# Expert output rows kept in DRAM per pass and fetched per token in the last pass, in a two-layer trunk

## What is computed

```
for l in range(2):
    x = x + hybrid_mixer(rmsnorm(x, attn_norm[l]), ...)
    h = rmsnorm(x, ffn_norm[l])
    if l == 0: x = x + (silu(h @ w_gate) * (h @ w_up)) @ w_down        # width 2816
    else:
        top_logit, top_e = top_k(h @ w_router + b_router, 2)           # 8 experts
        top_w = softmax(top_logit)
        for each token t, each of its two experts e with weight w:      # width 1408
            x[t] += w * ((silu(h[t] @ w_gate[e]) * (h[t] @ w_up[e])) @ w_down[e])
```

## Time and profile before

| | |
|---|---|
| median of 3 runs | 1048.85 us (1046.59 to 1050.11) |
| the profiled execution | 1049.15 us, its span 1047.4 us |
| mean granted PE clock | 0.998 of 2.4 GHz |
| busy PE, DVE, ACT, POOL | 98%, 80%, 62%, 3% of the span |
| DMA | 248.74 MB, mean 237 GB/s |
| HBM read, written | 246.99 MB, 1.05 MB |
| passes 0 to 7 of the experts | about 632 to 1037 us of the span |

### The profile page before, as it was taken

How to read it: one execution, slowest core, us unless ns; L and a number is a source line. 1 busy time by engine, 2 the same in 40 slices (tenths; PEclk the granted TensorE clock), 3 DMA queues, 4 the chain that set the end, 5 groups by cost and what they waited for, 6 DMA issues and landing times.

```text
span 1047.4 us, 14339 instructions
## 1 busy us (share of the span) xinstructions
PE 1026.5 (98%) x5058; PEld 867.8 (83%) x5058; DVE 833.5 (80%) x1165; ACT 653.0 (62%) x896; POOL 27.9 (3%) x75
## 2 busy tenths in 40 slices
PE   7999999999999999999999999999999999999997
PEld 6888788878888897888888877889888988898885
DVE  5799887765554556689887768999999999999986
ACT  6658655554343444657655556776877677777864
POOL 6000000040000000000000000000000000000000
PEclk9999999999999999999999999999999999999999
DMA  9735545675655554634555476999999989998992
GB/s 269 239 107 187 172 155 189 213 243 182 203 187 187 195 181 130 199 101 161 170 172 174 147 281 205 313 356 329 334 360 335 352 306 368 341 348 304 380 336 86
DMA packets 115093, 248.74 MB, mean 237 GB/s; under 512 B 4913, under 2 KB 29555, under 8 KB 115041
## 3 DMA queue, kind: packets, MB, share of 16 engines
q1 hardware_dynamic: 113040, 243.55, 67.7%
q0 software_dynamic: 2000, 4.51, 1.8%
HBM read 246.99 MB, written 1.05 MB: 237 GB/s over the span
## 4 chain that ended last, share of the span: by engine, by line
PE 87%; DVE 7%; ACT 2%; DMA 2%; issue 1%; SPq 0%; DVEq 0%; ACTq 0%
PE bank L369 26%; PE bank L371 26%; PE bank L370 26%; DVE wlo L357 2%; DMA ring<-in_w_in 2%; PE bank L981 1%; ACT whi L350 1%; DVE dacc L1593 1%; DVE h L1387 1%; PE bank L920 1%; DVE x L1385 1%; PE bank L917 1%; PE bank L941 1%; PE bank L942 1%; DMA ring<-in_moe_w_gate 1%
## 5 line engine op out<-in xcount | busy, mean ns | idle before, releaser
L357 DVE TENSOR_TENSOR wlo<-ring,whi 128x1024 fp32r<-128x1024 f32 (+2 forms) x506 | 540.1, 1120 | 94.1 <-ACT whi L350 92.0
L350 ACT CAST whi<-ring 128x1024 fp32r<-128x1024 f32 (+2 forms) x506 | 462.7, 972 | 86.3 <-PE bank L371 75.0
L369 PE MATMUL bank<-whi,hTh 128*128 128x512 f32 (+3 forms) x992 | 376.2, 379 | 2.7 <-DVE hTl L1362 1.3
L371 PE MATMUL bank<-whi,hTl 128*128 128x512 f32 (+3 forms) x992 | 370.9, 374 | 0.0
L370 PE MATMUL bank<-wlo,hTh 128*128 128x512 f32 (+3 forms) x992 | 370.6, 374 | 0.0
L369 PEld LDWEIGHTS bank<-whi,hTh 128*128 128x128 f32 x992 | 186.8, 188 | 34.0 <-issue 2.0
L371 PEld LDWEIGHTS bank<-whi,hTl 128*128 128x128 f32 x992 | 186.6, 188 | 29.2
L370 PEld LDWEIGHTS bank<-wlo,hTh 128*128 128x128 f32 x992 | 186.9, 188 | 28.5 <-issue 0.5
L369 PE MATMUL bank<-whi,oTh 128*128 128x512 f32 x392 | 155.0, 395 | 0.0
L371 PE MATMUL bank<-whi,oTl 128*128 128x512 f32 x392 | 153.0, 390 | 0.0
L370 PE MATMUL bank<-wlo,oTh 128*128 128x512 f32 x392 | 152.8, 390 | 0.0
(11 more groups left out here) (301 smaller groups left out, 736.2 us busy)
## 6 DMA issues: line engine op xcount, KB each, us to landing
ring<-in_w_in SPq DMA_DIRECT2D x40, 1024.0 KB, 5.2
ring<-in_moe_w_down SPq DMA_DIRECT2D x40, 1024.0 KB, 6.6
ring<-in_moe_w_gate SPq DMA_DIRECT2D x32, 1024.0 KB, 7.7
ring<-in_moe_w_up SPq DMA_DIRECT2D x32, 1024.0 KB, 8.5
ring<-in_moe_w_gate SPq DMA_DIRECT2D x16, 768.0 KB, 7.8
ring<-in_moe_w_up SPq DMA_DIRECT2D x16, 768.0 KB, 4.5
ring<-in_ffn_w_gate SPq DMA_DIRECT2D x11, 1024.0 KB, 5.1
ring<-in_ffn_w_up SPq DMA_DIRECT2D x11, 1024.0 KB, 5.3
```

The lines of the kernel that those rows point to most:

```text
L350: nc.scalar.copy(whi[pc.part(hf)][:, 0:n], pc.raw[:, hf * n:(hf + 1) * n]).then_inc(hi_done, 1)
L357: nc.vector.tensor_tensor(wlo[q][:, 0:n], pc.raw[:, hf * n:(hf + 1) * n], whi[q][:, 0:n].bitcast(F32), ALU.subtract).then_inc(lo_done, 1)
L369: nc.tensor.matmul(o, sh, wh, start=start, stop=False)
L371: return nc.tensor.matmul(o, sl, wh, start=False, stop=stop)
```

## The change

The expert's output rows of a pass are no longer multiplied back to tokens in the next pass. ACT copies banks 0 and 1, without weights, into `ystage` (the tile `gain`, free by then), and SP writes it (512 KB) to a tensor in DRAM, between the fetches of pieces 7 and 8 of the next pass. POOL first fills the rows of passes 7 to 11 with ones (five DMAs), and in the last pass, once the rows of pass 6 have landed, fetches each token's two rows by four indirect DMAs of 128 rows of 4 KB, into the tiles `htokh` and `htokl` (free by then). DVE adds them to `x` with the tokens' weights (`add_rows`). For that it computes each token's row numbers and weights in pass 0 (`token_rows`, 17 instructions; a row that the last pass makes gets the weight 0 here). Only the last pass still goes through slot_rows, rows_upper, rows_lower, scatter and scattered.

```diff
@@ tiles (build_trunk)
+        hotw = place("hotw", [P, MT, NE])
...
+        rowmark = place("rowmark", [P, 1])
@@ aliases and the tensor in DRAM
+        ystage = gain
+        yrows = nc.dram_tensor("yrows", (PASSES * P, D), F32).ap()
+        ypass = yrows.rearrange("(e p) d -> e p d", p=P)
+        tokrow = [[t[:, m, :].bitcast(F32) for m in range(MT)] for t in (htokh, htokl)]
@@ SP
-            def expert_stream(p, e):
+            def expert_stream(p, e, first=False):
...
+                    if j == ERING + 2 and not first:
+                        sp.wait_ge(y_hi, 2 * p)
+                        sp.dma_start(ypass[bass.ds(p - 1, 1), :, :].rearrange("e p d -> (e p) d"),
+                                     ystage[:, :]).then_inc(y_out, 16)
...
-            with sp.Fori(0, NE - 1) as p:
+            expert_stream(0, 0, first=True)
+            with sp.Fori(1, NE - 1) as p:
                 expert_stream(p, p)
...
+            sp.wait_ge(fill_in, 16 * (PASSES - NE + 1))
...
-            sp.wait_ge(sca_add, 4 * last_pass + 4)
+            sp.wait_ge(sca_add, 4)
@@ POOL, after load_gain(3)
+            for e in range(NE - 1, PASSES):
+                pool.dma_start(ypass[e].rearrange("p (k c) -> p k c", c=P),
+                               ones[:, :].unsqueeze(1).to_broadcast([P, D // P, P])).then_inc(fill_in, 16)
+            pool.wait_ge(fill_in, 16 * (PASSES - NE + 1))
+            pool.wait_ge(trow_ready, 1)
+            pool.wait_ge(rows_landed, 1)
+            for c in range(2):
+                for m in range(MT):
+                    pool.indirect_dma_start(tokrow[c][m], None, yrows,
+                                            bass.IndirectOffsetOnAxis(ap=trowi[:, c, m:m + 1], axis=0)
+                                            ).then_inc(tokrow_in, 16)
@@ PE: slot_rows(side) and scatter() lose the pass number (waits on 1 and 2)
@@ PE, down_part
                         if st == 0 and not first:
-                            pe.wait_ge(sca_add, 4 * before + 2)
+                            pe.wait_ge(y_hi, 2 * before + 2)
@@ PE, expert_pass
                     if kind == "u" and part and st == 0:
-                        if not first:
-                            scatter(before)
-                        slot_rows(q, side)
+                        if not more:
+                            slot_rows(side)
                         turn(0)
@@ ACT, expert_pass
-                    rows_upper(before)
+                    rows_out(before)
...
+                    if kind == "g" and part and st == 1 and not more:
+                        act_e.wait_ge(y_out, 16 * before + 16)
+                        nc.scalar.copy(rowmark[:, :], eps[:, :]).then_inc(rows_landed, 1)
...
-                        act_e.wait_ge(pick_mm, p + 1)
-                        nc.scalar.copy(pickT[:, :], bank[7][:, 0:T]).then_inc(pickT_ev, 1)
+                        if not more:
+                            act_e.wait_ge(pick_mm, 1)
+                            nc.scalar.copy(pickT[:, :], bank[7][:, 0:T]).then_inc(pickT_ev, 1)
...
+                if not first and more:
+                    act_e.wait_ge(y_out, 16 * before + 16)
+
+            def rows_out(q):
+                act_e.wait_ge(w_used, 2 * (MOE_BASE + PASS_PIECES) + 2 * PASS_PIECES * q)
+                for c in range(2):
+                    nc.scalar.copy(ystage[:, 512 * c:512 * (c + 1)], bank[c][:, :]).then_inc(y_hi, 1)
@@ DVE, router_weights: the weighted one-hot goes to hotw, hot is kept
@@ DVE, new
+            def token_rows():
...
+            def add_rows():
+                dve.wait_ge(tokrow_in, 16 * 2 * MT)
+                for c in range(2):
+                    for m in range(MT):
+                        last = V.scalar_tensor_tensor(out=x[:, m, :], in0=tokrow[c][m], scalar=tweight[:, c, m:m + 1],
+                                                      in1=x[:, m, :], op0=ALU.mult, op1=ALU.add)
+                    link(last)
@@ DVE, expert_pass
-                    rows_lower(before)
+                    if not more:
+                        pick_rows(q, side)
...
                         turned(0)
-                        if not first:
-                            scattered(before, 0)
-                        dve.wait_ge(pickT_ev, p + 1)
-                        V.tensor_copy(wslot[:, :], bank[7][:, T:T + 1]).then_inc(wslot_ready, 1)
-                    if kind == "g" and part == 0 and st == 1 and not first:
-                        scattered(before, 1)
+                        if not more:
+                            dve.wait_ge(pickT_ev, 1)
+                            V.tensor_copy(wslot[:, :], bank[7][:, T:T + 1]).then_inc(wslot_ready, 1)
                     if kind == "d" and part == 0 and st == 0:
                         if side and more:
                             pick_tokens(q + 1)
-                            pick_rows(q + 1)
                         if first:
                             second_passes()
+                            token_rows()
+                        if not more:
+                            add_rows()
@@ DVE, pick_rows(q, side) makes one side (2 pickf and 2 wcol, not 4 and 4); the calls left
             router_weights()
-            pick_rows(0)
             expert_pass(0, 0, 0)
```

More of the change, by code:

```diff
@@ L235, in build_trunk @@
         hot = place("hot", [P, 2, MT, NE])
+        hotw = place("hotw", [P, MT, NE])
+        rprod = place("rprod", [P, 2, MT, NE])
+        oprod = place("oprod", [P, 2, MT, NE])
+        trank = place("trank", [P, 2, MT])
+        tover = place("tover", [P, 2, MT])
+        tpass = place("tpass", [P, 2, MT])
+        trow = place("trow", [P, 2, MT])
+        tkeep = place("tkeep", [P, 2, MT])
+        tweight = place("tweight", [P, 2, MT])
+        trowi = place("trowi", [P, 2, MT], I32)
+        rowmark = place("rowmark", [P, 1])
         prod = place("prod", [P, 3, 6, NE])
@@ L319, in build_trunk @@
         sca_mm, sca_add = sem("sca_mm"), sem("sca_add")
+        y_out, fill_in, rows_landed, trow_ready, tokrow_in = sem("y_out"), sem("fill_in"), sem("rows_landed"), sem("trow_ready"), sem("tokrow_in")
         class Piece:
@@ L921, in gather, with slot_rows @@
                 last.then_inc(gat_mm, 1)
-            def slot_rows(q, side):
-                if side == 0:
-                    pe.wait_ge(rows_ready, q + 1)
+            def slot_rows(side):
+                pe.wait_ge(rows_ready, 1)
                 for m in range(MT):
@@ L932, in slot_rows, with scatter @@
                 last.then_inc(pick_mm, 1)
-            def scatter(q):
-                pe.wait_ge(y_lo, 2 * q + 2)
+            def scatter():
+                pe.wait_ge(y_lo, 2)
                 for m in range(MT):
@@ L1030, in _ @@
             expert_pass(2 * rounds + 1, rounds, 1, before=2 * rounds, more=False)
-            scatter(2 * rounds + 1)
+            scatter()
         @block.scalar
@@ L1305, in rows_upper @@
                 act_e.wait_ge(w_used, 2 * (MOE_BASE + PASS_PIECES) + 2 * PASS_PIECES * q)
-                act_e.wait_ge(wslot_ready, q + 1)
+                act_e.wait_ge(wslot_ready, 1)
                 for c in range(2):
@@ L1787, in router_weights @@
                 for m in range(MT):
-                    last = V.tensor_scalar(hot[:, 0, m, :], hot[:, 0, m, :], wtop[:, m, 0:1], None, ALU.mult)
+                    last = V.tensor_scalar(hotw[:, m, :], hot[:, 0, m, :], wtop[:, m, 0:1], None, ALU.mult)
                 link(last)
@@ L1791, in router_weights @@
                     last = V.scalar_tensor_tensor(out=tab[:, 4 + m, 0:NE], in0=hot[:, 1, m, :], scalar=wtop[:, m, 1:2],
-                                                  in1=hot[:, 0, m, :], op0=ALU.mult, op1=ALU.add)
+                                                  in1=hotw[:, m, :], op0=ALU.mult, op1=ALU.add)
                 link(last)
@@ L1878, in pick_tokens, with pick_rows @@
                 last.then_inc(pick_ready, 1)
[L1880 to L1887, removed]
+            def pick_rows(q, side):
+                for m in range(MT):
+                    rank = tab[:, m, bass.ds(2 * q + side, 1)]
+                    member = tab[:, 2 + m, bass.ds(2 * q + side, 1)]
+                    V.tensor_scalar(pickf[:, m, side, :], iotaf[:, :], rank, member, ALU.is_equal, ALU.mult)
+                    last = V.tensor_copy(wcol[:, side, m:m + 1], tab[:, 4 + m, bass.ds(2 * q + side, 1)])
                 last.then_inc(rows_ready, 1)
@@ L1900, in rows_lower, with scattered @@
                                            in1=yh[:, o].bitcast(F32), op0=ALU.mult, op1=ALU.subtract).then_inc(y_lo, 1)
-            def scattered(q, m):
+            def scattered(m):
                 for c in range(2):
-                    dve.wait_ge(sca_mm, 4 * q + 2 * m + c + 1)
+                    dve.wait_ge(sca_mm, 2 * m + c + 1)
                     o = x[:, m, 512 * c:512 * (c + 1)]
@@ L1936, in _ @@
             for m in range(MT):
-                scattered(2 * rounds + 1, m)
```

(1 more changed line is left out.)

20 lines of the change are left out of this document (added).

## The result

The changed kernel takes **1053.08 us**, median of 6 runs (1052.47 to 1053.91), the kernel before 1048.32 in 6 runs: a ratio of 1.0048, 95% interval 1.0037 to 1.0059. It is slower by about 5 us, where 2 us faster was forecast, and it lies 0.08 us past the upper end of the range.

A forecast was written before the change was run, and what follows sets the result against it. PE, busy 98% of the span, was taken as the bound, with DVE and the DMA queue close behind. Terms -7.0 - 1.0 + 2.3 + 1.4 + 2.2 = -2.1 us gave 1046.8 us against the 1048.85 median; range 1042.5 to 1053.

The forecast's parts named there:

- the wait in the last pass: Last pass, DVE ahead of add_rows: waits for the four gathers, landing at 1017.4 while DVE comes at about 1016; +1.4 us.
- rival C: Last pass: gathers come late, POOL taking 2 us for each, the last landing near 1022; 1051.8 us, chance 0.10.
- Scatter and slot_rows, -7.0: Passes 1 to 7: PE work leaves, but turn(0) then waits for DVE's eact, PE idle 1.4 us; -7.0 us (-2 to -9).
- Start of pass 0, -1.0: Pass 0: pick_rows(0) leaves the front of DVE's run, shortening PE's 1.91 us wait for eact; -1.0 us (-0.6 to -1.3).
- rival B: Better covers: shorter wait in pass 0 keeps the clock up (-1.6), gathers land before DVE comes (-1.4); 1043.8 us, chance 0.20.
- `token_rows`, +2.3: Pass 0: 17 DVE operations behind second_passes, ahead of turn(2), which nothing covers; +2.3 us (1.5 to 3).
- `add_rows`, +2.2: Last pass: four DVE operations, 5.0 us, ahead of lower parts PE needs, less 2.8 of cover; +2.2 us (1 to 4).
- SP's writes, the queue, the fills, each 0: Row writes hidden by 4 us to spare in the passes' DMA queue, POOL's five fills by queue share at 410 us; 0 each.
- A: Passes 1 to 7: clock falls after each 1.4 us wait ahead of turn(0), 1.6 us each; 1058.0 us, chance 0.12.
- D: Passes: the DMA queue becomes the bound, writes among reads costing 5 us each instead of 1.3; 1051.3 us, chance 0.05.
- E: Whole kernel: the change does nothing that counts, no part reaches PE; 1048.85 us, chance 0.03.
- the tail: After pass 7, at the kernel's end: claimed to stay the same.

The follow-up runs named there:

- x3: The changed kernel with each of the four indirect DMAs replaced by a plain one of the same size, adding wrong rows: 1049.99 us, one run.
- x2: The changed kernel without the four indirect DMAs and DVE's wait for them; add_rows stays, output lacks the experts' rows of passes 0 to 6: 1045.06 us.
- x1: The changed kernel with add_rows and DVE's wait for the gathered rows moved to the end of the last pass, just before rows_lower: 1043.39 us.
- x5: x1 with token_rows also moved from pass 0 into the last pass: 1041.33 us.
- x6: The kernel before with only turn(0) moved, in every pass, behind the first piece of the next step's gate products: 1045.34 us.
- x7: x5 with turn(0) also moved, in every pass, behind the first piece of the next step's gate products: 1028.89 us.
- x9: The changed kernel with ACT's mark that releases POOL's gathers moved one group of products earlier, behind pickT; add_rows stays: 1045.04 us.
- x10: The changed kernel with only turn(0) moved behind the first piece of the next step's gate products: 1040.47 us.
- x4: The changed kernel without writes, fills, gathers, token_rows and add_rows; scatter and slot_rows stay out of passes 0 to 6: 1039.84 us.
- x8: x4 with turn(0) moved behind the first piece of the next step's gate products: 1026.98 us.

## Why the prediction was wrong

**The step that failed** is the wait in the last pass, "+1.4 (0 to 5)". It measured 7.6 us. The working had 10.4 us from the mark to the last landing (3.0 fixed, 5.4 and 2.0 of queue); it took 17.3 (999.71 to 1017.02). DVE came 9.7 us after the mark, near the 9 of the working. The prediction's own sign for rival C, a DVE wait over 3 us before `add_rows`, is what the trace shows. Two things were wrong in the 10.4, and x3 tells them apart: with plain DMAs the 10.4 are 13.4 (999.53 to 1012.96), so 3.0 of the missing 6.9 us lie in the queue and 3.9 in the indirect form.

- **POOL's own time was put at nothing** in the forecast. It is 6.3 us from the first issue to the last, where x3's plain DMAs need 1.6, and 3.9 us of the wait are gone there. Rival C said this, in almost these numbers ("if POOL takes 2 us for each": 1.7 and 0.3), at a chance of 0.10. The trace of before has no indirect DMA, and I let the plain one stand for it. With no row for an operation, C deserved more than 1 in 10.
- **The queue was read from one window.** I used 1007 to 1013 of the kernel before, 0.62 at 174 GB/s, and put the transfers of 512 KB at the 4.3 us of a calm stretch. But the transfers run on for 22 us after turn(0), up to 1024 on the clock of before, and this is what the kernel before does there (windows, columns as in the earlier trace rows):

```profile
1012.00:1016.00 4.00, 4.00 (x19) 3.30 (x19) 4.00 (x5) 2.75 (x4) 0.00 (x0) 1.00 0.96 290
1016.00:1020.00 4.00, 4.00 (x23) 3.48 (x22) 3.52 (x5) 1.57 (x3) 0.00 (x0) 1.00 1.03 416
1020.00:1024.00 4.00, 4.00 (x25) 4.00 (x24) 3.96 (x5) 3.34 (x6) 0.00 (x0) 1.00 1.01 375
```

  My window lay on the one dip. The changed kernel has no such dip: 998 to 1015 is full throughout, 1.04 at 392 GB/s, and it isn't the gathers that fill it, for x2, which has none, shows 1.04 at 382 GB/s in the same stretch. The last transfer took 9.9 us, and the last plain one in x3 11.0. The Trainium skill (DMA: Bandwidth & Descriptors, Anatomy of one DMA) has 2.0 us plus the bytes at 436 GB/s, 3.2 us for 512 KB; these runs don't agree, with 6.4 to 11.0 us in a full queue.

A third part was in no term: the clock. It fell to 0.50 (1.2 GHz) at about 1019.6, while PE stood its 8.89 us, and came back at 1026.4; the products at 1023.65 take 0.52 us where 0.34 is usual. Of the 10.6 us 8.9 are PE's idle time and 1.7 are what is left, nearly all of it this clock (half speed over 3.2 us of work). At the end of the kernel, too, the scatter's pairs of products are 0.89 us apart where before they were 0.46, behind the same idle time of 2.22: +1.1. PE slowed there in x1, x2, x5, x6, x7, x9 and x10 too, and not in before, x3, x4 and x8, though the idle time is 2.22 us in all four of these and in x2, x6, x9 and x10 as well. So it doesn't go with the removal of the scatter. The clock moves between executions of one kernel too: those of the kernel before with a mean clock of 0.996 spanned 1047.3 to 1048.3 us, those with 0.999 1045.1 to 1046.0. The cause is open, and this +1.1 can't be put down to the change.

**The other terms**, by their own steps:

- **Scatter and slot_rows, -7.0**: measured -6.05, 0.86 for a pass. The mechanism was right in all its parts: `eact` is late next, the two plain copies take 1.08 us against 1.27 (0.19, as worked out), PE stands 1.45 us (1.4). x4 shows it without the rest, x7 and x8 what stood behind it.
- **Start of pass 0, -1.0**: measured -1.0. The wait there is 1.45 us and no longer 1.91, and the clock stayed at 1.00: 1.6 us more, which I had only under rival B, at 0.20 for both its halves.
- **`token_rows`, +2.3**: measured +2.4, and 2.1 came back in x5.
- **`add_rows`, +2.2**: measured 2.3 in x2.
- **SP's writes, the queue, the fills, each 0**: right (there are seven writes, not six: the last pass has one too; the fills landed after 8.2 us, median). x7 carries writes, fills and gathers, x8 none, and turn(0) of the last pass starts at 982.62 in the one and 982.63 in the other. The 1.9 us between their times (2.7 between the spans of the profiled executions) lie behind that: 1.0 up to turn(2), where PE waits 0.81 for `eact`, 0.8 ahead of the last scatter, behind `add_rows`, and in the profiled x7 about 1 us of slower clock in the scatter.

**The rivals.** A fell: the clock stayed at 1.00 in passes 1 to 6 behind idle times of 1.45 us. The Trainium skill (TensorE: Matmul & The Clock Gate, HAM oscillation) warns of gaps that return in each turn of a loop; no pass here shows a fall. B's first half came true (1.6 us), its second did not. C was the right one, and its price, 1051.8, was 1.3 us short, for it left the full queue and the clock out. D fell: x7 has the writes in and its passes take 48.3 us on average, the same as without them. E fell.

In sum: up to the last pass -5.7 was forecast and -6.25 measured (without the 0.8 ahead of pass 0), for the last pass +3.6 and +10.6, for the tail 0 and +1.1; together -2.1 and +5.5.

## What to carry to other kernels

Where work leaves the bounding engine, look at what it covered: here one DVE result was ready 1.45 us late in each pass, and of the 18.4 us that the removal is worth when that result is covered (x6 to x8) only 8.7 came out when it was not (x4); one piece of other work put between that result and its use gave the rest. A transfer that is issued in a stretch where weights stream at 390 GB/s, as here, should be given 10 us to land, and its issuer's time counted besides; put the use of it where the engine idles anyway, not at a wait in the middle of an in-order list with the bound engine's operands behind it.

## What was not expected of the hardware

- An indirect DMA of 128 rows of 4 KB took POOL 0.94 to 1.97 us, with 0.30 between two; a plain one of the same bytes took 0.55.
- With the queue full in the last pass a DMA of 512 KB from POOL landed 6.4 to 11.0 us after its issue, plain or indirect, and the writes of the rows from SP after 10.0 (median); none of them delayed a weight piece enough for PE to show it.
- PE at full load stood 1.45 us in seven places without a fall of the granted clock; 1.91 us at the start of pass 0 (before) and 8.89 us (after) were followed by 0.50 over about 3 us of work, 5.02 us (x3) by 0.50 over 6 us of work. Behind 2.22 us ahead of the last scatter it fell in five kernels (after, x2, x6, x9, x10) and not in four (before, x3, x4, x8), and behind about 3.0 us there it fell in all three (x1, x5, x7).
